# Forgetting-attention stages: weight splits in quarters, one a tile, and the square sums of queries and keys issued last at a tile's end

## The chip, the cores and the metric

One core of a Trainium2 chip runs the whole program. The metric is the device time of one execution in microseconds (us), the median of the runs. The engines, as the profile names them: PE (TensorE; PEld is its weight load), DVE (VectorE), ACT (ScalarE), POOL (GpSimd), SP (SyncE, which issues the weight transfers).

## What is computed

A first block of four layers works on 272 tokens (16 learned ones and 256 of the input) of width 1024, a second block of two layers on the 256. Layers 0 and 3 of the first block have the mixer that the change touches, "fox" in the names:

```python
def fox_mixer(h, w_in, b_f, q_gain, k_gain, w_out):
    proj = h @ w_in
    q, k, v, gate, f = jnp.split(proj, [D_MODEL, 2 * D_MODEL, 3 * D_MODEL, 4 * D_MODEL], axis=-1)
    q = rmsnorm(q.reshape(B, L, H, Dh), q_gain) * (Dh ** -0.5)      # 16 heads of 64
    k = rmsnorm(k.reshape(B, L, H, Dh), k_gain)
    c = jnp.cumsum(jax.nn.log_sigmoid(f + b_f), axis=1)
    # softmax(q k^T + c_q - c_k, causal) v, per head
    o = o * jax.nn.sigmoid(gate)
    return o @ w_out
```

All is fp32. The large products run as three products of rounded halves: weight and activation are each split into a high part (rounded to fp32r) and a low part (the rest), and high x high, high x low and low x high are summed in PSUM.

## The kernel before, in words

**Weights.** `stream()` lists the weight stages in order: `fox_in0` (8 blocks of 4 tiles), `fox_out0` (2 blocks), `gu0`, `dn0` and so on; `fox_in1` comes after `dn2`. A tile is 128 output features: 8 chunks of 128 rows, each with three matmuls of 128x272, 24 in all. A block is loaded in two halves of 2048 columns into a ring of four slots. ACT rounds a half into `ring_hi` (`split`, ACT's part, L1464), DVE subtracts and writes `ring_lo` (`split`, DVE's part, L1994). `hooks` decides when: a half of the next block at the tiles t with t % 4 = 0 and 2, so at every even tile. PE waits on `lo_ready` ahead of each half of a block.

**A fox_in stage.** `FOX_TILES` puts the 32 tiles in the order q, k, v of head pair 0, q, k, v of head pair 1, ..., then the 8 gate tiles. So head pair c has the tiles t = 3c (query), 3c + 1 (key) and 3c + 2 (value). Attention of the pairs is done between the tiles: five units a pair, called A (two, 144 keys), B (two, 272 keys) and M (16 learned tokens), in the slots 3c + 4, 3c + 5 and 3c + 6. Each engine has its own list in program order and none overtakes.

- PE, after tile t (`after`): the scores of the units in slot t; then, if tile t - 1 was a query or key tile, `statistic`, the sum of its squares over the 64 features of a head (the matmul `ps<-sq,con`); then `turn`, which transposes the probabilities of the units in slot t - 1; then `values`, their products with v, for slot t - 2. `statistic` writes PSUM bank 7, which holds one sum at a time: the one for keys waits on `head_ready`, that is until DVE is through with the query sum of the same pair. Half-way through a tile (`middle`) PE transposes a pair's values into the same bank.
- DVE, at tile t: `inverse` (reciprocals of slot t - 1); `head_norm` of tile t - 2 if it is a query or key tile (three `newton` steps L2010 to L2012 on `hrs`, then two products, L2092); the split hook; `evacuate` (tile t from PSUM times `rstd`, L2120); `largest` (row maxima of the scores of slot t, L2129).
- ACT, at tile t: `rstd_of` tile t - 2 (a logarithm and an exponential into `hrs`, L1464); copies of transposed probabilities (`take_turned`, slot t - 2) and of values (`take_tokens`); the split hook; the square of tile t; `exponent` of slot t. At tile 1 it also runs `log_sigmoid` with two table loads.
- POOL multiplies probabilities by the reciprocals.

At the end PE waits until the last gate tile has left PSUM (`all_read`) and goes on with `fox_out`. Two PSUM banks hold the tiles of this stage, so PE may start tile t + 2 only when tile t is evacuated.

## Time and profile before

| | |
|---|---|
| median of 3 runs | 2488.18 us (2487.27 to 2494.31) |
| profiled execution | 2484.18 us, span 2482.6 us |
| PE busy, share of the span | 93% |
| DVE, ACT, POOL busy | 63%, 49%, 25% |
| mean granted TensorE clock | 0.977 of full speed |
| first fox_in stage | PE starts at 23.05 us, the out stage at 205.89 us |
| second fox_in stage | ends at 1451.68 us |

Times in a timeline row are start and length of an instruction in us; what stands in brackets is how long the engine was idle just before it, and who ended that. PE's matmuls overlap, so starts tell its pace better than lengths.

### The profile page before, as it was taken

The numbers are of one execution on the slowest core, as the hardware profiler recorded it, in microseconds if no ns is written. First come the engines' busy times: TensorE is split into PE (matmuls) and PEld (weight loads), VectorE is DVE, ScalarE is ACT, GpSimd is POOL, SyncE is SP. The second block draws the span as 40 slices with busy tenths as digits, with TensorE's granted clock in tenths as the row PEclk, the third lists the DMA queues.
The fourth block names the chain that finished last, engine by engine and source line by source line (L and its number), as shares of the span: only waits on it lengthen the run. The fifth ranks groups of instructions, "written<-read, shape, count | busy, mean of one in ns | idle before, by whom it ended". The sixth has DMA issues, their size and how long they took to land. (4 is left out here: it accounts for less than half of the span.)

```text
span 2482.6 us, 47467 instructions
## 1 busy us (share of the span) xinstructions
PE 2303.6 (93%) x19122; PEld 2180.4 (88%) x19122; DVE 1555.4 (63%) x2514; ACT 1212.9 (49%) x1861; POOL 626.7 (25%) x774
## 2 busy tenths in 40 slices
PE   5999999999999898799989999997899998899998
PEld 4878999889999787699988789996788998788998
DVE  4665554746654764565556656546657975666994
ACT  4555544545444642355345554443446554456553
POOL 3114211013211030032121142216034535024550
PEclk9999999999999898899999999999999999999999
DMA  4324545324545212155442345454253554243554
GB/s 164 103 86 146 177 158 190 128 85 142 180 156 167 89 67 69 37 173 181 156 150 86 103 136 170 162 183 147 94 181 132 188 164 160 86 136 120 187 172 134
DMA packets 52859, 343.99 MB, mean 139 GB/s; under 512 B 5904, under 2 KB 7120, under 8 KB 20176
## 3 DMA queue, kind: packets, MB, share of 16 engines
q1 hardware_dynamic: 51984, 336.26, 41.0%
q0 software_dynamic: 704, 5.31, 0.5%
q8 instruction: 125, 2.05, 0.3%
q14 instruction: 46, 0.38, 0.0%
HBM read 340.43 MB, written 1.05 MB: 138 GB/s over the span
## 5 line engine op out<-in xcount | busy, mean ns | idle before, releaser
L740 PE MATMUL ps<-arena_r,ring_hi 128*128 128x272 f32 (+1 forms) x6688 | 1602.7, 289 | 16.8 <-DVE arena L2120 7.4
L740 PEld LDWEIGHTS ps<-arena_r,ring_hi 128*128 128x128 f32 x6688 | 1171.7, 191 | 26.8 <-issue 10.4
L740 PE MATMUL ps<-y_r,ring_hi 128*128 128x272 f32 (+1 forms) x3424 | 1019.9, 298 | 50.2 <-DVE ring_lo L1994 23.1
L740 PE MATMUL ps<-y_r,ring_lo 128*128 128x272 f32 (+1 forms) x3424 | 985.1, 288 | 0.0
L1994 DVE TENSOR_TENSOR ring_lo<-ring,ring_hi 128x2048 fp32r<-128x2048 f32 (+1 forms) x348 | 737.2, 2120 | 389.4 <-ACT ring_hi L1464 388.9
L740 PEld LDWEIGHTS ps<-y_r,ring_hi 128*128 128x128 f32 x3424 | 655.7, 192 | 79.5 <-issue 39.5
L740 PEld LDWEIGHTS ps<-y_r,ring_lo 128*128 128x128 f32 x3424 | 657.1, 192 | 0.0
L1464 ACT ACTIVATE ring_hi<-ring 128x2048 fp32r<-128x2048 f32 (+1 forms) x348 | 607.6, 1747 | 101.3 <-DMA ring<-dn 46.3
L740 PE MATMUL ps<-arena_r,ring_lo 128*128 128x272 f32 (+1 forms) x1632 | 468.3, 287 | 0.0
L740 PEld LDWEIGHTS ps<-arena_r,ring_lo 128*128 128x128 f32 x1632 | 310.1, 190 | 0.0
L1464 ACT ACTIVATE arena<-arena 128x272 f32<-128x272 f32 (+7 forms) x199 | 93.4, 472 | 404.1 <-DVE arena L2553 268.8
L2855 POOL CAST arena_r<-arena 128x272 fp32r<-128x272 f32 (+1 forms) x132 | 135.0, 1023 | 543.1 <-DVE arena L2555 420.2
L740 PE MATMUL ps<-arena 64*64 64x64 f32 (+16 forms) x2856 | 223.5, 264 | 21.7 <-DMA arena<-arena 6.1
L740 PEld LDWEIGHTS ps<-arena 64*64 64x64 f32 (+9 forms) x2856 | 160.8, 145 | 63.0 <-issue 34.6
L2863 POOL TENSOR_SCALAR arena<-x,par 128x272 f32<-128x272 f32 (+1 forms) x112 | 97.6, 871 | 380.7 <-ACT y_r L1464 380.0
L1464 ACT ACTIVATE sq<-x 128x272 f32<-128x272 f32 (+1 forms) x120 | 50.7, 423 | 236.7 <-DVE x L2032 236.7
L1464 ACT ACTIVATE arena<-ps 128x256 f32<-128x256 f32 (+7 forms) x299 | 92.7, 360 | 93.7 <-PE ps L740 37.1
L2032 DVE TENSOR_TENSOR x<-ps,x 128x272 f32<-128x272 f32 (+1 forms) x112 | 48.4, 432 | 100.2 <-PE ps L740 99.7
L2847 POOL CAST arena_r<-arena 128x256 fp32r<-128x256 f32 (+1 forms) x40 | 21.4, 534 | 335.0 <-DVE arena L2660 171.1
L2856 POOL TENSOR_TENSOR arena_r<-arena,arena_r 128x272 fp32r<-128x272 f32 (+1 forms) x132 | 103.0, 781 | 10.6
L1464 ACT ACT_TABLE_LOAD x69 | 88.5, 1283 | 23.1 <-DMA ring<-fox_in 9.3
L2594 DVE SCALAR_TENSOR_TENSOR arena<-arena,par 128x256 f32<-128x256 f32 x176 | 99.6, 624 | 0.0
(234 smaller groups left out, 1707.4 us busy)
## 6 DMA issues: line engine op xcount, KB each, us to landing
ring<-gu SPq DMA_DIRECT2D x88, 1024.0 KB, 5.0
ring<-dn SPq DMA_DIRECT2D x64, 704.0 KB, 4.0
ring<-up SPq DMA_DIRECT2D x44, 1024.0 KB, 5.0
ring<-fox_in SPq DMA_DIRECT2D x32, 1024.0 KB, 5.1
ring<-sdn SPq DMA_DIRECT2D x32, 704.0 KB, 4.0
ring<-gdn_in SPq DMA_DIRECT2D x16, 1024.0 KB, 5.0
ring<-in SPq DMA_DIRECT2D x16, 1024.0 KB, 5.1
ring<-gla_in SPq DMA_DIRECT2D x12, 1024.0 KB, 5.1
```

What stands on the lines that cost most here:

```text
L740: return nc.tensor.matmul(dst, w, mv, start=start, stop=stop)
L1464: return nc.scalar.activation(dst, src, f, **kw)
L1994: V.tensor_tensor(ring_lo[:, slot, 0:w], ring[:, slot, 0:w], ring_hi[:, slot, 0:w].bitcast(F32), ALU.subtract).then_inc(lo_ready, 1)
L2032: V.tensor_tensor(dst[:, c, :], take(c, width), dst[:, c, :], ALU.add).then_inc(evacuated, 1)
L2594: V.scalar_tensor_tensor(out=u_cc[:, q, :], in0=u_gp[:, q, 1 + tap:1 + tap + SEQ], scalar=par[:, bass.ds(i * 24 + (w0 + 12 * b + 3 * q + 1 ...
L2847: step(G.tensor_copy(hi_r[:, c, :], lo[:, c, :]))
L2855: step(G.tensor_copy(hi_r[:, c, :], lo[:, c, :]))
L2856: G.tensor_tensor(lo_r[:, c, :], lo[:, c, :], hi_r[:, c, :].bitcast(F32), ALU.subtract).then_inc(h_split, 1)
L2863: step(G.tensor_scalar(lo[:, c, :], src[:, c, :], pcol(gain, c), 1.0, ALU.mult, ALU.mult))
```

## The change

Fox_in stages split a quarter of a block (1024 columns) at every tile instead of a half (2048) at every even tile. All other stages still split halves. `hi_ready` and `lo_ready` now count quarters everywhere (a half counts two), and PE waits ahead of each quarter in all stages. In `after`, `statistic` moves behind `turn` and `values`.

```diff
+        def share(g, part):
+            w = half_width[g]
+            return slice(0, w) if part is None else slice(part * w // 2, (part + 1) * w // 2)
+        def quarters(at, part):
+            return 2 * at + (2 if part is None else part + 1)
-        def hooks(split, n, tpb):
+        def hooks(split, n, tpb, fine):
             def at(t):
                 g = n.block + t // tpb + 1
                 if g < len(half_width):
-                    if t % tpb == 0:
-                        split(g, 0)
-                    if t % tpb == tpb // 2:
-                        split(g, 1)
+                    if not fine:
+                        if t % tpb == 0:
+                            split(g, 0)
+                        if t % tpb == tpb // 2:
+                            split(g, 1)
+                    elif t % (tpb // 4) == 0:
+                        quarter = t % tpb // (tpb // 4)
+                        split(g, quarter // 2, part=quarter % 2)
...
-                            if at == 0:
-                                pe.wait_ge(lo_ready, i * (2 * turn) + (2 * (n.block + b) + half + 1))
+                            for part in range(2):
+                                if 0 <= at + P - 1 - part * width_of_half // 2 < P:
+                                    pe.wait_ge(lo_ready, i * (4 * turn) + quarters(2 * (n.block + b) + half, part))
...
                     for u in in_slot(units, t):
                         scores(u)
-                    if t:
-                        part, c = FOX_TILES[t - 1]
-                        if part in "qk":
-                            statistic(part, c)
                     for u in in_slot(units, t - 1):
                         turn(u)
                     slot = in_slot(units, t - 2)
                     if slot:
                         values(slot)
+                    if t:
+                        part, c = FOX_TILES[t - 1]
+                        if part in "qk":
+                            statistic(part, c)
...
-                fn(ring_hi[:, slot, 0:w], ring[:, slot, 0:w], ACT.Copy).then_inc(hi_ready, 1)
+                fn(ring_hi[:, slot, cols], ring[:, slot, cols], ACT.Copy).then_inc(hi_ready, 2 if part is None else 1)
...
-                before = hooks(split, n, tpb)
+                before = hooks(split, n, tpb, name.startswith("fox_in"))
...
-                V.tensor_tensor(ring_lo[:, slot, 0:w], ring[:, slot, 0:w], ring_hi[:, slot, 0:w].bitcast(F32),
-                                ALU.subtract).then_inc(lo_ready, 1)
+                V.tensor_tensor(ring_lo[:, slot, cols], ring[:, slot, cols], ring_hi[:, slot, cols].bitcast(F32),
+                                ALU.subtract).then_inc(lo_ready, 2 if part is None else 1)
...
-                after = hooks(split, n, tpb)
+                after = hooks(split, n, tpb, name.startswith("fox_in"))
```

On DVE, at tiles 11, 12 and the start of 13 of a fox_in stage, the list of before (line numbers of the kernel before; `newt` and `hrs` are `head_norm`, `raw` and the first `arena<-ps,rstd` are `evacuate`):

```order
89 L2092 SCALAR_TENSOR_TENSOR arena<-raw,gain,hrs 64x272 x2
90 L2120 TENSOR_TENSOR arena<-ps,rstd 128x272
...
98 L2012 SCALAR_TENSOR_TENSOR hrs<-newt,hrs 128x272
99 L2092 SCALAR_TENSOR_TENSOR arena<-raw,par,hrs 64x272 x2
100 L1994 TENSOR_TENSOR ring_lo<-ring,ring_hi 128x2048
101 L2120 TENSOR_TENSOR raw<-ps,rstd 128x272
...
104 L2139 RECIPROCAL row_inv<-row_sum 64x1
105 L2120 TENSOR_TENSOR raw<-ps,rstd 128x272
```

and of the changed kernel, where L2009 is the split and L2135 is `evacuate`:

```order
94 L2107 SCALAR_TENSOR_TENSOR arena<-raw,gain,hrs 64x272 x2
95 L2009 TENSOR_TENSOR ring_lo<-ring,ring_hi 128x1024
96 L2135 TENSOR_TENSOR arena<-ps,rstd 128x272
...
104 L2027 SCALAR_TENSOR_TENSOR hrs<-newt,hrs 128x272
105 L2107 SCALAR_TENSOR_TENSOR arena<-raw,par,hrs 64x272 x2
106 L2009 TENSOR_TENSOR ring_lo<-ring,ring_hi 128x1024
107 L2135 TENSOR_TENSOR raw<-ps,rstd 128x272
...
110 L2154 RECIPROCAL row_inv<-row_sum 64x1
111 L2009 TENSOR_TENSOR ring_lo<-ring,ring_hi 128x1024
112 L2135 TENSOR_TENSOR raw<-ps,rstd 128x272
```

One split of 2048 columns ahead of one of three evacuations has become a split of 1024 ahead of each.

On PE, at the end of tile 11, before and then after (`arena 128x272` are the scores B, L924 and L939 are `turn`, `arena 64x16` is `values` of M, `sq,con` is `statistic`):

```order
357 L740 MATMUL ps<-arena 128x272 x2
358 L740 MATMUL ps<-sq,con 128x272
359 L924 MATMUL ps<-con,arena 128x128
...
363 L740 MATMUL ps<-arena 64x16 x2
364 L740 MATMUL ps<-y_r,ring_hi 128x272
```

```order
357 L753 MATMUL ps<-arena 128x272 x2
358 L939 MATMUL ps<-con,arena 128x128
...
362 L753 MATMUL ps<-arena 64x16 x2
363 L753 MATMUL ps<-sq,con 128x272
364 L753 MATMUL ps<-y_r,ring_hi 128x272
```

The square sum, which stood directly behind the scores, now stands directly ahead of the next tile.

On DVE, at the last four gate tiles, before and then after (L2145 and L2160 multiply by the gate, L2150 and L2165 are a late split of the attention output):

```order
224 L1994 TENSOR_TENSOR ring_lo<-ring,ring_hi 128x2048
225 L2120 TENSOR_TENSOR arena<-ps,rstd 128x272
226 L2145 TENSOR_TENSOR arena<-arena 128x272 x5
227 L2120 TENSOR_TENSOR arena<-ps,rstd 128x272
228 L2145 TENSOR_TENSOR arena<-arena 128x272
229 L1994 TENSOR_TENSOR ring_lo<-ring,ring_hi 128x2048
230 L2120 TENSOR_TENSOR arena<-ps,rstd 128x272
231 L2145 TENSOR_TENSOR arena<-arena 128x272
232 L2150 TENSOR_TENSOR arena_r<-arena,arena_r 128x272
233 L2120 TENSOR_TENSOR arena<-ps,rstd 128x272
```

```order
238 L2009 TENSOR_TENSOR ring_lo<-ring,ring_hi 128x1024
239 L2135 TENSOR_TENSOR arena<-ps,rstd 128x272
240 L2160 TENSOR_TENSOR arena<-arena 128x272 x5
241 L2009 TENSOR_TENSOR ring_lo<-ring,ring_hi 128x1024
242 L2135 TENSOR_TENSOR arena<-ps,rstd 128x272
243 L2160 TENSOR_TENSOR arena<-arena 128x272
244 L2009 TENSOR_TENSOR ring_lo<-ring,ring_hi 128x1024
245 L2135 TENSOR_TENSOR arena<-ps,rstd 128x272
246 L2160 TENSOR_TENSOR arena<-arena 128x272
247 L2165 TENSOR_TENSOR arena_r<-arena,arena_r 128x272
248 L2009 TENSOR_TENSOR ring_lo<-ring,ring_hi 128x1024
249 L2135 TENSOR_TENSOR arena<-ps,rstd 128x272
```

A quarter now stands ahead of the last evacuation too, where no split stood.

## Rows read from the trace of the kernel before

**Rows 1.** The page, parts 1 and 5: busy time, and the split on DVE.

```profile
PE 2303.6 (93%) x19122; PEld 2180.4 (88%) x19122; DVE 1555.4 (63%) x2514; ACT 1212.9 (49%) x1861; POOL 626.7 (25%) x774
...
L1994 DVE TENSOR_TENSOR ring_lo<-ring,ring_hi 128x2048 fp32r<-128x2048 f32 (+1 forms) x348 | 737.2, 2120 | 389.4 <-ACT ring_hi L1464 388.9
```

**Rows 2.** PE's waits, 20 to 210 us: total, times, longest.

```profile
PE ps L740 <- DVE arena L2092: 9.1, 4, 2.8
```

**Rows 3.** PE's waits, 1277 to 1455 us (second stage), same columns.

```profile
PE ps L740 <- DVE arena L2092: 10.8, 4, 4.5
```

**Rows 4.** PE's timeline, the waiting square sums: start, length, instruction, idle before.

```profile
96.60 0.92 PE L740 MATMUL ps<-sq,con 128*128 128x272 f32 x2 [2.06 <-DVE arena L2092]
...
132.15 0.70 PE L740 MATMUL ps<-sq,con 128*128 128x272 f32 x2 [2.11 <-DVE arena L2092]
...
166.17 0.70 PE L740 MATMUL ps<-sq,con 128*128 128x272 f32 x2 [2.10 <-DVE arena L2092]
...
1343.90 0.70 PE L740 MATMUL ps<-sq,con 128*128 128x272 f32 x2 [2.12 <-DVE arena L2092]
...
1411.95 0.70 PE L740 MATMUL ps<-sq,con 128*128 128x272 f32 x2 [2.10 <-DVE arena L2092]
```

**Rows 5.** DVE's timeline, tiles 10 to 12 of the first stage.

```profile
89.25 2.29 DVE L1994 TENSOR_TENSOR ring_lo<-ring,ring_hi 128x2048 fp32r<-128x2048 f32 x1 [3.05 <-ACT ring_hi L1464]
91.46 0.43 DVE L2120 TENSOR_TENSOR raw<-ps,rstd 128x272 f32<-128x272 f32 x1
...
94.02 0.44 DVE L2010 SCALAR_TENSOR_TENSOR newt<-ps,hrs 128x272 f32<-128x272 f32 x1 [0.67 <-ACT hrs L1464]
...
96.49 0.44 DVE L2120 TENSOR_TENSOR arena<-ps,rstd 128x272 f32<-128x272 f32 x1
...
99.31 0.44 DVE L2010 SCALAR_TENSOR_TENSOR newt<-ps,hrs 128x272 f32<-128x272 f32 x1 [0.67 <-ACT hrs L1464]
...
102.02 2.29 DVE L1994 TENSOR_TENSOR ring_lo<-ring,ring_hi 128x2048 fp32r<-128x2048 f32 x1 [0.27 <-ACT ring_hi L1464]
```

**Rows 6.** ACT's timeline, the same stretch.

```profile
85.92 1.49 ACT L1464 ACTIVATE arena<-ps 128x256 f32<-128x256 f32 x6
87.32 1.90 ACT L1464 ACTIVATE ring_hi<-ring 128x2048 fp32r<-128x2048 f32 x1
91.93 0.43 ACT L1464 ACTIVATE sq<-raw 128x272 f32<-128x272 f32 x1 [2.71 <-DVE raw L2120]
...
105.33 0.94 ACT L1464 ACTIVATE arena<-ps 128x256 f32<-128x256 f32 x4
```

**Rows 7.** Timelines of ACT and DVE around a split of 1024 columns (stage in2b).

```profile
1746.45 1.04 ACT L1464 ACTIVATE ring_hi<-ring 128x1024 fp32r<-128x1024 f32 x1
...
1747.53 1.23 DVE L1994 TENSOR_TENSOR ring_lo<-ring,ring_hi 128x1024 fp32r<-128x1024 f32 x1 [1.43 <-ACT ring_hi L1464]
1748.67 0.41 DVE L2647 CUSTOM_DVE_ANT_0 arena<-ps,arena 128x256 f32<-128x256 f32 x1
```

**Rows 8.** Busy time by stretch: span, then PE, PEld, DVE, ACT, POOL, clock, DMA.

```profile
96.60:102.60 6.00, 6.00 (x34) 5.05 (x35) 4.27 (x13) 4.63 (x12) 0.98 (x2) 0.72 0.23 96
132.15:136.63 4.48, 4.48 (x34) 3.94 (x34) 3.04 (x11) 3.73 (x12) 0.99 (x2) 1.00 0.30 123
```

**Rows 9.** Timelines at a stage's start: DVE, ACT (first stage), DVE (both stages).

```profile
34.84 2.29 DVE L1994 TENSOR_TENSOR ring_lo<-ring,ring_hi 128x2048 fp32r<-128x2048 f32 x1 [0.29 <-ACT ring_hi L1464]
...
38.23 0.43 ACT L1464 ACTIVATE arena<-arena 16x272 f32<-16x272 f32 x1 [0.29 <-DVE arena L2081]
...
62.76 0.44 DVE L2120 TENSOR_TENSOR arena<-ps,rstd 128x272 f32<-128x272 f32 x1
...
1309.63 0.44 DVE L2120 TENSOR_TENSOR arena<-ps,rstd 128x272 f32<-128x272 f32 x1 [1.39 <-PE ps L740]
```

**Rows 10.** DVE's timeline, evacuation of gate tiles 28 and 31, first stage.

```profile
192.43 0.43 DVE L2120 TENSOR_TENSOR arena<-ps,rstd 128x272 f32<-128x272 f32 x1
...
205.41 0.42 DVE L2120 TENSOR_TENSOR arena<-ps,rstd 128x272 f32<-128x272 f32 x1
```

13 lines of the change are left out of this document (7 added, 6 removed).

## The prediction

> **What bounds the kernel now.** I read the busy shares first, then PE's waits in the two fox_in stages, then the timelines of PE, DVE and ACT there. PE is busy 93% of the span, DVE 63%, and the split on DVE is its largest group [rows 1]. So the kernel is bound by PE, and an edit that adds no PE work can win only where PE stands still. In the two stages that the change touches PE waits for `head_norm` (L2092) 9.1 and 10.8 us, four times each [rows 2, 3]. The first of the four comes at tile 2; the other three are 2.1 us each, always at a key sum, at tiles 11, 17 and 23, thus with every second head pair [rows 4].
>
> The three gaps recur at a fixed distance: 132.15 to 166.17 is 34.02 us, and 1343.90 to 1411.95 is two times 34.03 [rows 4]. PE's own work in such a stretch of six tiles is 34.02 - 2.10 = 31.92 us, 15.96 a head pair. The question that decides the prediction is whether only one late link makes the gap, or whether the whole round of DVE and ACT takes 34 us.
>
> I add the round up. DVE and ACT hand work to each other in program order, so each step is the distance between two starts. ACT's half 1.93 (87.32 to 89.25), DVE's half 2.21 (89.25 to 91.46), evacuation to the next one with a query `head_norm` between 5.03 (91.46 to 96.49) [rows 5, 6]; evacuation of the value tile to the next split 5.53 (96.49 to 102.02), which would be 2.82 + 2.47 = 5.29 if ACT's half were ready (96.49 to 99.31, and `head_norm` itself 94.02 to 96.49) [rows 5]; half 2.21; from there to ACT's copies 1.10 (105.33 less 104.23, where 104.23 is 102.02 + 2.21) [rows 5, 6]; copies 1.40 (85.92 to 87.32) [rows 6]. The next head pair has no split ahead of its key evacuation, which runs while ACT copies: 5.03 less the 0.47 from evacuation to square (91.46 to 91.93) is 4.56 [rows 5, 6]; then half 2.21, 5.29, 1.10 and 1.40. Sum 33.97 us. Measured are 34.02 and 34.03. **So in these stages the round between DVE and ACT sets the pace, not PE**, and the gap at each second key sum is only where PE notices. What was shortened at one place must shorten this sum, or PE waits elsewhere.
>
> **The change part by part.**
>
> *Quarters in the middle of a stage.* A quarter costs 1.08 us on ACT until DVE may start, and 1.14 on DVE (1746.45 to 1747.53 to 1748.67) [rows 7]. The new list has one ahead of each of the three evacuations. At the query and value tiles ACT's quarter is covered, since `head_norm` takes 2.47 us meanwhile; at the key tile, behind the copies, it is not. Round of one head pair: 1.08 + 1.14 + 5.03 + 1.14 + 5.29 + 1.14 + 1.10 + 1.40 = 17.32 us, two pairs 34.64. That is 0.62 longer than the 34.02 measured: two quarters cost 0.07 more than a half on DVE (three times), the key evacuation with its 0.47 is never free any more, and ACT's time on the path stays (2.16 against 1.93 + 0.24). The order that let one split per two pairs hide behind the tile's own wait is gone. PE then stands still 17.32 - 15.96 = 1.4 us in every pair instead of 2.1 in every second.
>
> *The square sum last.* It fills PE's wait with `turn` and `values`, and this would be a gain if PE set the pace. Under a round of DVE and ACT it moves work from behind the wait to before it and changes nothing but at tile 24, where the last round ends. Who waits for the later sum: ACT's `rstd_of`, for the query sum. ACT asks for it only behind the evacuation, the square and the exponents of the key tile, and that evacuation now stands 1.08 + 1.14 = 2.2 us behind ACT's copies, where it stood beside them. So I cost it at 0; bounds 0 and +0.5 a head pair, the latter if `values` still waits for ACT's copies when the sum is due.
>
> *From tile 5 to 23, first stage.* Evacuation at 62.76 [rows 9] to the one at 96.49 is 33.73, becomes 34.64: +0.91. 96.60 to 132.15 is 35.55, because the clock was at half speed for part of it: 6.00 us at a granted clock of 0.72 for what takes 4.48 at 1.00, so 1.5 us [rows 4, 8]. In the new round PE has 1.4 us to spare in a pair and such a spell costs about 0.1, so 34.64: -0.91. 132.15 to 166.17: +0.62. *Second stage.* At 1309.63 DVE waited 1.39 us for PE [rows 9], and the new quarter of 1.14 falls into that wait: 34.15 to 1343.78 becomes about 33.5, -0.6; then 68.05 becomes 69.28: +1.2.
>
> *Start of a stage.* DVE waited 0.29 for ACT's half at 34.84; with quarters it goes on at 34.55, evacuates at 35.69, ACT squares at 36.16, is free at 36.49, and has the quarter of tile 1, which did not stand there, until 37.56. The chain of `log_sigmoid` that started at 38.23 starts there: -0.67 [rows 5 to 7, 9]. It leads to PE's first key sum. I take the same in the second stage; bounds -1.2 and 0, since the quarter at tile 1 is queued ahead of that chain.
>
> *End of a stage.* From the evacuation of tile 28 to that of tile 31, on which `all_read` waits, are 12.98 us [rows 10]. Tile 28: a quarter in place of a half on both engines, 0.85 + 1.07, less 0.5 because ACT arrives later: -1.4. Tile 29: a new quarter on DVE, +1.14. Tile 30: -1.92. Tile 31: a quarter on both engines where none was, of which ACT's part is half covered, +1.6. Together -0.6 a stage, bounds -1.4 and +1.0.
>
> *More waits in PE's list.* Each half has one more wait, in all stages. The low part is written about a block ahead of its use, and in these stages PE's waits name `ring_lo` nowhere behind the first tile, so 0; bounds 0 and +1 us for the whole kernel. SP's transfers hang on PE's tiles and are not moved.
>
> The sum: first stage -0.67 + 0.91 - 0.91 + 0.62 - 0.6 = -0.65; second -0.67 - 0.6 + 1.2 - 0.6 = -0.65; together -1.3 us. Against the profiled execution this is 2484.18 - 1.3; the median of the runs stands 4.0 above that execution, so I put it on the median: **2486.9 us**. The terms' bounds give -5 to +5.
>
> **The rivals.**
>
> *The gaps close.* If the round had slack that my sum doesn't see, halving what stands ahead of the key evacuation brings `head_norm` forward by 0.85 + 1.07 = 1.9 us and the work now ahead of the sum fills the rest, so all six gaps of 2.1 go: -12.6, with the spell of half clock -1.5, starts -1.3, ends -1.2: 2471.6. For it: DVE is busy only 63%, and a half does stand ahead of the evacuation at 91.46, from which `head_norm` and the key sum at 96.60 follow [rows 4, 5]. Against it: the sum of the round meets the measured distance within 0.1 us, and the new round is longer. The Trainium skill, page "Perfetto Trace Analysis", section "Optimizing Scalar/DVE Operations", says that where Scalar and Vector are not saturated but cause bubbles elsewhere, breaking up instructions may let work complete sooner. By that rule this rival would be the forecast; by the rows, the pieces are all on the same path and their sum is what counts. The same section says that each instruction has a fixed overhead; the rows give that as 2 x 1.14 against 2.21. Chance 0.15.
>
> *Many small gaps cool PE.* The key sums of all pairs now wait, some eleven in the two stages instead of six. If each is followed by a spell of half clock as the one at 96.60 was, and PE cannot absorb it, each costs 1.5 us: ten more, +15, 2503. It decides where 15.96 + 1.52 = 17.48 passes the round of 17.32, so as I see it the price is 0.16 and not 1.5; and four of the five gaps in rows 4 show full pace behind them. It needs the spell to fall where DVE waits for PE. Chance 0.07.
>
> *The change does nothing.* Splits in quarters but the same round: within the forecast's range.
>
> **How the numbers follow.** Forecast 0.78, closing gaps 0.15, cooling 0.07. About 0.3%, 7.5 us, can be told from no change here. The forecast case lies between 2480 and 2494, the upper part for spells of half clock that fall otherwise in later stages. To hold 8 in 10 I stretch the low end into the first rival, to 2473. Faster: 0.15 and a small part of the forecast case, 0.18. Slower 0.07. Same 0.75.
>
> **What would show it.** Right: PE's waits for `head_norm` become six or more a stage of about 1.4 us and their sum stays near 9 us; key sums stand 17.3 us apart; each of DVE's quarters is 1.2 us. The distance from tile 5's evacuation to the sum at tile 23 grows. Wrong: key sums 16 us apart with no idle before them (closing gaps), or a granted clock under 1.00 behind most of them (cooling), or a wait for `ring_lo` that stood nowhere in these stages.

## The result: slower by 0.3%, through TensorE's granted clock

The changed kernel takes 2499.45 us (median of 20 runs, 2488.8 to 2509.54), the kernel before beside it 2492.99 (20 runs). The ratio is 1.0032, 95% interval 1.0018 to 1.0045. I had forecast no change, 2486.9 us, and gave 0.07 to slower. Of the 12.6 us between forecast and result 4.8 are the base: I had put the forecast on 2488.18, a median of three runs, where twenty give 2492.99. The rest is 1.3 us of gain that I had forecast and 6.5 us of loss.

The page of the changed kernel, part 1, and the two lists of PE's waits that answer to [rows 2] and [rows 3]: total, times, longest. The stretches are 20 to 210 and 1277 to 1465 us.

```profile
PE 2319.1 (93%) x19122; PEld 2198.3 (88%) x19122; DVE 1559.6 (62%) x2546; ACT 1215.1 (49%) x1893; POOL 627.0 (25%) x774
```

```profile
PE ps L753 <- DVE arena L2107: 6.0, 6, 2.6
PE ps L753 <- DVE arena L2135: 4.4, 2, 3.7
PE ps L939 <- ACT arena L1479: 3.8, 6, 0.7
```

```profile
PE ps L753 <- DVE arena L2107: 8.1, 6, 4.8
...
PE ps L939 <- ACT arena L1479: 3.5, 6, 0.7
```

PE issues the same 19122 matmuls as before [rows 1] but is busy 15.5 us longer. Its waits for `head_norm` (L2107, formerly L2092) are shorter than in [rows 2, 3], 6.0 and 8.1 us for 9.1 and 10.8, and new ones for ACT (3.8 and 3.5) stand beside them; all of PE's waits together come to 0.5 us more in the first stage and 1.2 us more in the second (18.3 to 19.5 from the key sum at tile 2 on). So the lost time is not idle time in the two stages that were changed. PE's timeline there, key sums of both stages, answers to [rows 4]:

```profile
96.58 0.70 PE L753 MATMUL ps<-sq,con 128*128 128x272 f32 x2 [0.68 <-DVE arena L2107]
101.12 0.85 PE L939 MATMUL ps<-con,arena 128*128 128x128 f32 x6 [0.66 <-ACT arena L1479]
113.75 0.70 PE L753 MATMUL ps<-sq,con 128*128 128x272 f32 x2 [0.67 <-DVE arena L2107]
130.93 0.70 PE L753 MATMUL ps<-sq,con 128*128 128x272 f32 x2 [0.69 <-DVE arena L2107]
148.10 0.70 PE L753 MATMUL ps<-sq,con 128*128 128x272 f32 x2 [0.68 <-DVE arena L2107]
165.26 0.70 PE L753 MATMUL ps<-sq,con 128*128 128x272 f32 x2 [0.66 <-DVE arena L2107]
```

```profile
1355.94 0.70 PE L753 MATMUL ps<-sq,con 128*128 128x272 f32 x2 [0.68 <-DVE arena L2107]
...
1424.62 0.70 PE L753 MATMUL ps<-sq,con 128*128 128x272 f32 x2 [0.67 <-DVE arena L2107]
```

Every pair now waits, and they stand 17.17 us apart: the round of DVE and ACT sets the pace, as argued. The time is lost elsewhere, in the stages named GLA and GDN here, the mixers of layers 1 and 2. Busy time by stretch: the program from PE's first matmul to the start of the GLA stage; then 132 matmuls at the start of that stage; then the stretch from the GDN stage to the end of that layer. Columns are span, PE busy (instructions), granted clock, DMA share, GB/s. First the kernel before, then the changed one:

```profile
23.06:435.28 412.22, 392.71 (x3025) 0.99 0.41 135
435.28:453.22 17.94, 17.94 (x132) 1.00 0.28 86
728.76:1120.22 391.46, 355.35 (x3803) 0.95 0.32 105
```

```profile
23.05:434.56 411.51, 391.48 (x3025) 0.99 0.41 136
434.56:454.05 19.49, 19.48 (x132) 0.91 0.24 73
731.28:1131.82 400.54, 363.61 (x3803) 0.92 0.31 102
```

Everything up to 435 us, with the first changed stage in it, has become 0.71 us shorter. Then come 132 matmuls of a stage that the diff leaves as it was but for its counting: the same work, no idle, 1.55 us longer at a granted clock of 0.91. The GDN stretch costs 9.1 us more at 0.92 against 0.95; this second difference will turn out to be scatter of single profiles. What the clock does there can be read in PE's timeline of the changed kernel, where the distance of the starts goes from 0.13 to 0.23 us with no wait in between, thus to the lower of the two levels (1.2 GHz for 2.4):

```profile
444.01 0.29 PE L753 MATMUL ps<-y_r,ring_lo 128*128 128x272 f32 x1
444.14 0.32 PE L753 MATMUL ps<-y_r,ring_hi 128*128 128x272 f32 x1
444.26 0.43 PE L753 MATMUL ps<-arena_r,ring_hi 128*128 128x272 f32 x1
444.48 0.43 PE L753 MATMUL ps<-y_r,ring_lo 128*128 128x272 f32 x1
444.71 0.43 PE L753 MATMUL ps<-y_r,ring_hi 128*128 128x272 f32 x1
```

**A measure for all runs.** A single profile can't carry a difference of 0.3% here, since the clock's low stretches fall differently in each execution. But every run reports its span and its mean granted clock. Their product is the time at full clock; the rest of the span I call *lost*. The clock is given to three places, worth 2.5 us, so only means count. And the split counts every stretch at the low clock as lost, also where PE would have waited for another engine anyway. One more run of the kernel before, 2598.92 us in a slower state, is left out. In the 151 others (five groups, each beside four or two of the experiments): full 2421.6 (standard error 0.25), lost 67.2 (0.6). The changed kernel: full 2421.0 (0.6), lost 76.7 (1.4). At full clock it is 0.6 us faster, within the error; it loses 9.5 us more to the clock. (The 20 runs of the kernel before that stand beside it have times alone on record, and their mean is 7.4 us under that of the changed kernel, in agreement within the errors.) So the whole loss is in the clock, and the question for the chip is which part of the change does it.

### The profile page after: what moved, and what is told of

It is laid out like the page before. It is cut to its first block and busy times, and to the rows that moved or that the text cites. A ratio compares the mean times of both kernels' runs of the same rounds, so it can differ in the third digit from the quotient of the medians.

```text
span 2500.6 us, 48406 instructions
## 1 busy us (share of the span) xinstructions
PE 2319.1 (93%) x19122; PEld 2198.3 (88%) x19122; DVE 1559.6 (62%) x2546; ACT 1215.1 (49%) x1893; POOL 627.0 (25%) x774
## 5 line engine op out<-in xcount | busy, mean ns | idle before, releaser
L753 PE MATMUL ps<-arena_r,ring_hi 128*128 128x272 f32 (+1 forms) x6688 | 1609.3, 290 | 16.6 <-DVE arena L2135 7.3
L753 PEld LDWEIGHTS ps<-arena_r,ring_hi 128*128 128x128 f32 x6688 | 1177.6, 192 | 27.4 <-issue 10.1
L753 PE MATMUL ps<-y_r,ring_hi 128*128 128x272 f32 (+1 forms) x3424 | 1027.6, 300 | 53.1 <-DVE ring_lo L2009 23.0
L2009 DVE TENSOR_TENSOR ring_lo<-ring,ring_hi 128x2048 fp32r<-128x2048 f32 (+2 forms) x380 | 742.4, 1955 | 412.5 <-ACT ring_hi L1479 411.0
L753 PE MATMUL ps<-y_r,ring_lo 128*128 128x272 f32 (+1 forms) x3424 | 990.6, 289 | 0.0
L753 PEld LDWEIGHTS ps<-y_r,ring_hi 128*128 128x128 f32 x3424 | 660.8, 193 | 81.8 <-issue 37.7
L1479 ACT ACTIVATE ring_hi<-ring 128x2048 fp32r<-128x2048 f32 (+2 forms) x380 | 613.6, 1615 | 110.8 <-DMA ring<-dn 50.3
L753 PEld LDWEIGHTS ps<-y_r,ring_lo 128*128 128x128 f32 x3424 | 662.8, 194 | 0.0
L753 PE MATMUL ps<-arena_r,ring_lo 128*128 128x272 f32 (+1 forms) x1632 | 468.9, 287 | 0.0
L753 PEld LDWEIGHTS ps<-arena_r,ring_lo 128*128 128x128 f32 x1632 | 310.6, 190 | 0.0
L753 PE MATMUL ps<-arena 64*64 64x64 f32 (+16 forms) x2856 | 224.7, 265 | 21.1 <-DMA arena<-arena 6.8
L753 PEld LDWEIGHTS ps<-arena 64*64 64x64 f32 (+9 forms) x2856 | 162.3, 145 | 62.4 <-issue 35.7
```

What stands on the lines that cost most here:

```text
L753: return nc.tensor.matmul(dst, w, mv, start=start, stop=stop)
L1479: return nc.scalar.activation(dst, src, f, **kw)
L2009: V.tensor_tensor(ring_lo[:, slot, cols], ring[:, slot, cols], ring_hi[:, slot, cols].bitcast(F32), ALU.subtract).then_inc(lo_ready, 2 if ...
```

## The experiments

The columns of this table: number of runs, ratio to the kernel before with its 95% interval, mean full and mean lost time in us (standard error of lost, 1.4 to 2.5).

| kernel | runs | ratio to before | full | lost |
|---|---|---|---|---|
| changed | 20 | 1.0032 [1.0018, 1.0045] | 2421.0 | 76.7 |
| e1 counting and extra waits | 11 | 1.0046 [1.0026, 1.0065] | 2421.2 | 78.2 |
| e2 changed, sums in the old place | 12 | 1.0031 [1.001, 1.0052] | 2420.8 | 73.8 |
| e3 sums last alone | 12 | 0.9988 [0.9972, 1.0004] | 2422.5 | 64.5 |
| e4 changed, extra waits in fox_in alone | 12 | 1.0022 [1.0004, 1.004] | 2422.2 | 71.3 |
| e5 before, one redundant wait a half | 12 | 1.0008 [0.999, 1.0027] | 2419.9 | 72.1 |
| e6 before, three redundant waits | 12 | 1.0001 [0.9982, 1.002] | 2420.1 | 69.5 |
| e7 counting alone | 9 | 1.0041 [1.0022, 1.0061] | 2421.9 | 76.9 |
| e8 changed, one wait a half | 12 | 1.0019 [0.9998, 1.0039] | 2421.5 | 71.0 |
| e9 lo_ready by twos | 12 | 1.0023 [1.0007, 1.0038] | 2420.7 | 75.7 |
| e10 hi_ready by twos | 12 | 0.999 [0.9972, 1.0008] | 2422.2 | 65.5 |
| e11 = e7 again | 12 | 1.0024 [1.0007, 1.0041] | 2424.4 | 71.4 |
| e12 changed, old counting | 10 | 0.9973 [0.9957, 0.999] | 2424.7 | 60.7 |
| e13 lo_ready and evacuated by twos | 7 | 1.0042 [1.0024, 1.0059] | 2423.3 | 76.8 |
| e14 evacuated by twos | 12 | 1.0038 [1.0023, 1.0054] | 2423.5 | 75.8 |
| e15 = e12 again | 12 | 0.9984 [0.9967, 1.0] | 2421.7 | 63.2 |
| e16 = e8 again | 12 | 1.0021 [1.0002, 1.0041] | 2421.4 | 72.5 |
| e17 lo_ready from an offset | 12 | 0.9994 [0.9981, 1.0007] | 2420.7 | 67.0 |
| e18 lo_ready by fours | 12 | 1.001 [0.9997, 1.0023] | 2422.4 | 69.6 |

### Which part of the change: e1 to e4

**e1**: the changed kernel with halves in all stages and the sums in the old place, so that only the counting in quarters and PE's extra waits are left.

```diff
-                before = hooks(split, n, tpb, name.startswith("fox_in"))
+                before = hooks(split, n, tpb, False)
...
-                after = hooks(split, n, tpb, name.startswith("fox_in"))
+                after = hooks(split, n, tpb, False)
```

> Halves everywhere and the old place of the square sums; only the counting in quarters and PE's additional waits are kept. Theory W (the additional waits in PE's list, which stand in all stages, cost time by themselves or by a lower granted clock in the mixer stages): 6 to 9 us slower than before, ratio near 1.003, and the mean clock 0.97 or less. Theory F (the loss comes from the fox_in stages alone): same as before within 2 us. Theory C (the later stages draw their spells of half clock by chance of timing, nothing in the change makes them more): same as before within 3 us.

**e2**: the changed kernel with `statistic` ahead of `turn` and `values` again.

```diff
+                    if t:
+                        part, c = FOX_TILES[t - 1]
+                        if part in "qk":
+                            statistic(part, c)
                     for u in in_slot(units, t - 1):
                         turn(u)
```

> Quarters and the additional waits, the square sums in their old place. By the sum of the prediction the round of a head pair stays 17.3 us, key sums 17.2 to 17.4 us apart, and the fox_in stages take what they take in the changed kernel, within 1 us. Theory W and theory F: 6 to 9 us slower than before. Theory C: within 3 us of before. If the place of the square sum matters after all: clearly different from the changed kernel.

**e3**: the kernel before with only the move of `statistic` behind `values`.

> Only the square sums moved; halves and waits as before. By the sum of the prediction the round of two head pairs stays 34.0 us and only tile 24 gains, 0.5 to 0.8 us a stage: 0 to -2 us. Theory W: same as before. Theory F, if the moved sums are what costs: 6 us or more slower.

**e4**: the changed kernel; blocks of the fox_in stages keep their two waits a half, all others wait once, for both quarters.

```diff
-                                if 0 <= at + P - 1 - part * width_of_half // 2 < P:
-                                    pe.wait_ge(lo_ready, i * (4 * turn) + quarters(2 * (n.block + b) + half, part))
+                                if n.block + b in in_quarters:
+                                    if 0 <= at + P - 1 - part * width_of_half // 2 < P:
+                                        pe.wait_ge(lo_ready, i * (4 * turn) + quarters(2 * (n.block + b) + half, part))
+                                elif at == 0 and part == 0:
+                                    pe.wait_ge(lo_ready, i * (4 * turn) + quarters(2 * (n.block + b) + half, 1))
```

> The changed kernel, but PE waits twice a half only for the blocks that are split in quarters; elsewhere once a half as before. Theory W: 6 to 9 us faster than the changed kernel, so 1 to 2 us faster than before. Theory F: like the changed kernel, 6 to 9 us slower than before. Theory C: within 3 us of before.

Measured: e1, which works in the fox_in stages exactly like the kernel before, has the whole loss, 78.2 us. e3, which has no new counting, has none. So the quarters and the late sums are not needed for the loss; the line of the diff that I had costed at nothing, counting and waits, is enough. e4 came out between the two and settled nothing. For the round, PE's timelines of e2 and then of e3 are worth reading:

```profile
96.78 0.70 PE L753 MATMUL ps<-sq,con 128*128 128x272 f32 x2 [1.17 <-DVE arena L2107]
...
113.95 0.70 PE L753 MATMUL ps<-sq,con 128*128 128x272 f32 x2 [1.18 <-DVE arena L2107]
```

```profile
101.00 0.70 PE L740 MATMUL ps<-sq,con 128*128 128x272 f32 x2 [1.46 <-DVE arena L2092]
...
135.10 0.70 PE L740 MATMUL ps<-sq,con 128*128 128x272 f32 x2 [1.44 <-DVE arena L2092]
```

With the sum in its old place the quarters give the same 17.17 us a pair (e2). With the sum late and halves as before, two pairs take 34.10 (e3) against 34.02 in [rows 4]. The late sum shortens the gap named at the key sum and does nothing for the round.

### The waits or the counting: e5 to e8

Theory W: the extra waits on PE lower the clock. Theory C: the counting by twos does.

**e5, e6**: the kernel before with one, and with three, redundant waits in each half, for a value that PE has already seen. This is e5; e6 has four parts in place of two.

```diff
-                            if at == 0:
-                                pe.wait_ge(lo_ready, i * (2 * turn) + (2 * (n.block + b) + half + 1))
+                            for part in range(2):
+                                if 0 <= at + P - 1 - part * (tpb * kc * P // 2) // 2 < P:
+                                    pe.wait_ge(lo_ready, i * (2 * turn) + (2 * (n.block + b) + half + 1))
```

> The kernel before with one redundant wait more on PE in the middle of each half of weights, for the same value of the semaphore that PE has already seen; counting, splits and sums as before. Of each run's time I take the span times the mean granted clock (the time at full clock, 2422.0 us for the kernel before) and what is left over (lost to the clock, 66.8 us before, 76.7 in the changed kernel). Theory W, the extra waits on PE take the clock down: lost 74 to 79 us, ratio to before 1.003 to 1.005. Theory C, the counting in quarters (increments of two, doubled values, other register arithmetic) does it: lost 64 to 69, ratio 0.999 to 1.001.

> The kernel before with three redundant waits more in each half. Theory W: more than with one, lost 80 to 100 us if the loss goes with the number of waits, ratio 1.006 to 1.014; 74 to 79 if one wait already does all of it. Theory C: lost 64 to 69, ratio 0.999 to 1.001. If the time at full clock grows too, a wait costs time of its own: up to 1 us by my prediction.

**e7**: e1 without its extra waits; **e8**: the changed kernel without them. Both have this at PE:

```diff
-                            for part in range(2):
-                                if 0 <= at + P - 1 - part * width_of_half // 2 < P:
-                                    pe.wait_ge(lo_ready, i * (4 * turn) + quarters(2 * (n.block + b) + half, part))
+                            if at == 0:
+                                pe.wait_ge(lo_ready, i * (4 * turn) + quarters(2 * (n.block + b) + half, 1))
```

> Halves and sums as in the kernel before, PE waits once a half as before, but the semaphores count quarters: each half adds two, and every value waited for is doubled. Theory W: lost 64 to 69 us, ratio 0.999 to 1.001. Theory C: lost 74 to 79 us, ratio 1.003 to 1.005.

> The changed kernel with its quarters and its late sums, but PE waits once a half, for the half's second quarter, in all stages. Theory W: the changed kernel without its loss: time at full clock 2421 us, lost 64 to 69, ratio to before 0.998 to 1.000, thus about where my prediction put the changed kernel. Theory C: lost 74 to 79, ratio 1.003, as the changed kernel. Either way the key sums of the fox_in stages stand 17.17 us apart, as in the changed kernel.

Measured: three redundant waits a half change nothing (1.0001), and one hardly anything (1.0008); the time at full clock is lower than before by 1.5 us, not higher. The counting without any extra wait has the loss, 76.9. So theory W has fallen as the cause of the whole. A share of a few us is not excluded: e5 lost 72.1 where the kernel before beside it lost 68.0, and e8, the changed kernel without the extra waits, lies between the groups at 71.0 against 76.7.

### Which semaphore, and can the change be had without it: e9 to e12

**e9** and **e10**: the kernel before with one of the two semaphores counted by twos, `lo_ready` (from DVE to PE) or `hi_ready` (from ACT to DVE). e9:

```diff
-                                pe.wait_ge(lo_ready, i * (2 * turn) + (2 * (n.block + b) + half + 1))
+                                pe.wait_ge(lo_ready, i * (4 * turn) + 2 * (2 * (n.block + b) + half + 1))
...
-                                ALU.subtract).then_inc(lo_ready, 1)
+                                ALU.subtract).then_inc(lo_ready, 2)
```

> The kernel before in which only lo_ready counts by twos: DVE's split adds two, PE waits for twice the value, and the register that PE multiplies for it in its loops is one of its own. Lost to the clock (span less span times mean granted clock) was 67 to 68 us in the kernel before and 76.9 with both semaphores doubled. If PE's own list of waits and register work is the cause (theory P), this kernel has all of it: lost 74 to 79, ratio 1.003 to 1.005. If it is the counting on ACT and DVE (theory D): 65 to 70, ratio 0.999 to 1.001. If the counting isn't a cause and e7 and e1 were drawn high by chance: 65 to 70 here, in the next kernel and in the third.

> The kernel before in which only hi_ready, between ACT and DVE, counts by twos; PE's list is word for word that of the kernel before. Theory P: lost 65 to 70 us, ratio 0.999 to 1.001. Theory D: 74 to 79, ratio 1.003 to 1.005.

**e11** is e7 once more.

> The kernel with the counting alone once more, on another day's runs and perhaps another chip, since single kernels differ in twelve runs by a standard error of 2 us. If counting lowers the clock: lost 74 to 79 us again, ratio 1.003 to 1.005, and a spell of half clock about 9 us into the first GLA stage, which the profiles of four kernels without the new counting don't have. If it was chance: lost 65 to 71.

**e12**: the changed kernel with its quarters and late sums, with PE's line and the values of both semaphores as in the kernel before. The first quarter of a half has a semaphore of its own between ACT and DVE and signals nothing to PE.

```diff
-                fn(ring_hi[:, slot, cols], ring[:, slot, cols], ACT.Copy).then_inc(hi_ready, 2 if part is None else 1)
+                fn(ring_hi[:, slot, cols], ring[:, slot, cols], ACT.Copy).then_inc(hi_first if part == 0 else hi_ready, 1)
...
-                v.wait_ge(hi_ready, i * 8 + quarters(at, part))
+                if part == 0:
+                    firsts.append(at)
+                    v.wait_ge(hi_first, len(firsts))
+                else:
+                    v.wait_ge(hi_ready, i * 4 + (at + 1))
...
+                if part != 0:
+                    low.then_inc(lo_ready, 1)
```

> The changed kernel with its quarters and late sums, but the old counting and PE's old waits: the first quarter of a half is signalled between ACT and DVE by a semaphore of its own, and only the second one counts for lo_ready. If the counting is the whole of the loss (P or D): time at full clock 2421 us, lost 65 to 70, total within 2486 to 2491, ratio 0.998 to 1.000, which is what I predicted for the changed kernel. If the quarters or the late sums cool PE too: lost above 72, ratio above 1.001.

Measured: `hi_ready` is innocent (65.5), `lo_ready` alone has the loss (75.7). e11 repeats e7 with a smaller loss, 71.4, between the two ranges that I had given. e12 is the opposite of the changed kernel with the same quarters and late sums: 0.9973, lost 60.7, lower than the 65 to 70 that I had expected. Its rows, key sums first, then the three stretches from above:

```profile
97.38 0.70 PE L754 MATMUL ps<-sq,con 128*128 128x272 f32 x2 [0.67 <-DVE arena L2115]
114.54 0.70 PE L754 MATMUL ps<-sq,con 128*128 128x272 f32 x2 [0.66 <-DVE arena L2115]
```

```profile
22.91:434.90 411.99, 393.14 (x3025) 0.98 0.41 135
434.90:452.83 17.93, 17.93 (x131) 1.00 0.29 90
728.49:1120.06 391.57, 355.30 (x3802) 0.95 0.32 105
```

The same pairs of 17.16 us, the same gaps of 0.67; but the GLA stage's first matmuls run at full clock again, and the GDN stretch is at 391.6.

### What it is in the counting: e13 to e18

Doubling `lo_ready` also changes PE's compiled list in the looped stages: by the traces PE executes 296 register instructions for 312. **e13** doubles `evacuated`, the other semaphore of these loops, as well, which brings back the 312 (e18 has them too); **e14** doubles `evacuated` alone.

```diff
-                        pe.wait_ge(evacuated, i * (turn * tpb) + (n.tile + t + 1 + BANKS - banks))
+                        pe.wait_ge(evacuated, i * (2 * turn * tpb) + 2 * (n.tile + t + 1 + BANKS - banks))
...
-            v.sem_inc(evacuated, BANKS)
+            v.sem_inc(evacuated, 2 * BANKS)
```

and every `then_inc(evacuated, 1)` adds two.

> The kernel before in which lo_ready and evacuated both count by twos. In PE's compiled list the register and wait instructions of the looped stages are then in the places of the kernel before again (three in 51 rows), where the doubling of lo_ready alone gave another list (two in 50 rows). If PE's list is the cause (theory R): lost to the clock 65 to 70 us, ratio 0.999 to 1.001, no spell of half clock 9 us into the first GLA stage. If the increments of two on lo_ready are (theory I): lost 74 to 79, ratio 1.002 to 1.005, the spell there.

> The kernel before in which only evacuated counts by twos; PE's list has the register and wait instructions of the kernel before. Theory R and theory I: lost 65 to 70 us, ratio 0.999 to 1.001, no spell in the first GLA stage. If any semaphore counted by twos does it: 74 to 79.

**e15** and **e16** are e12 and e8 once more.

> The kernel with quarters, late sums and the old counting once more, to see whether its gain holds: if the recounting was the whole loss, 0.998 to 1.000 with 65 to 70 us lost; in the first twelve runs it was 0.9973 with 60.7 lost, which is lower than any cause that I know of explains. No spell in the first GLA stage.

> The changed kernel with one wait a half once more. It has the register code of the looped stages that goes with lo_ready doubled, but its one profile had no spell at the start of the first GLA stage and its loss was 71.1 us, between the groups. If that code or counting lowers the clock: 72 to 78 lost, ratio 1.002 to 1.004. If the extra waits on PE of the changed kernel have a part: 65 to 70.

**e17**: `lo_ready` starts at an offset, so it has the large values but increments of one. **e18**: it counts by fours.

```diff
-                                pe.wait_ge(lo_ready, i * (2 * turn) + (2 * (n.block + b) + half + 1))
+                                pe.wait_ge(lo_ready, i * (2 * turn) + (len(half_width) * 2 + 2 * (n.block + b) + half + 1))
...
             v.sem_inc(evacuated, BANKS)
+            v.sem_inc(lo_ready, len(half_width) * 2)
```

```diff
-                                pe.wait_ge(lo_ready, i * (2 * turn) + (2 * (n.block + b) + half + 1))
+                                pe.wait_ge(lo_ready, i * (8 * turn) + 4 * (2 * (n.block + b) + half + 1))
...
-                                ALU.subtract).then_inc(lo_ready, 1)
+                                ALU.subtract).then_inc(lo_ready, 4)
```

> The kernel before in which lo_ready starts at the number of all halves and then counts by ones: as large values as with the doubling, increments of one, PE's list unchanged in form. If large values are the cause (theory V): lost to the clock 72 to 78 us, ratio 1.002 to 1.005, a spell of half clock 9 us into the first GLA stage. If increments of more than one are (theory I): lost 63 to 70, ratio 0.999 to 1.001, no such spell.

> The kernel before in which lo_ready counts by fours; PE's list has the same kinds of instructions in the same places as in the kernel before. Theory I: lost 72 us or more, with the spell in the first GLA stage; if the loss goes with the size of the increment, 85 us or more, ratio 1.006 and up. Theory V: the same, since the values are larger still. If what counts is only that PE's register instructions stood elsewhere (which the kernel with both semaphores doubled spoke against): lost 63 to 70, ratio 0.999 to 1.001.

Measured: with the old list and both semaphores doubled the loss is all there (76.8), so it isn't the register instructions. `evacuated` alone does it too (75.8), against both theories that I had named. The repeats: e15 has a gain again, smaller (0.9984, lost 63.2, below the 65 to 70 expected), and e16 lost 72.5, at the lower end of what the counting should give, above the 65 to 70 of the extra waits. Large values with increments of one do nothing (67.0). That left the increments; but by fours the loss is 69.6, ratio 1.001, and not the 72 or more that I asked for. So the size of the increment doesn't set it, and the increments as the cause are not shown.

**What an increment of more than one does to the program.** It is not only a number. The trace of the kernel before has no semaphore instruction at the line of the split's wait (L1993); those of e9 and e18 have 348 there, one for each split. The wait for `hi_ready`, which was part of the split, has become an instruction of its own ahead of it. Here are the first lines of the pages of the kernel before, e17, e9 and e18:

```profile
span 2482.6 us, 47467 instructions
```

```profile
span 2486.7 us, 47468 instructions
```

```profile
span 2499.0 us, 47791 instructions
```

```profile
span 2499.7 us, 47807 instructions
```

It costs time. ACT's half and DVE's split in the timelines of e9:

```profile
88.13 1.90 ACT L1464 ACTIVATE ring_hi<-ring 128x2048 fp32r<-128x2048 f32 x1
...
90.13 2.29 DVE L1994 TENSOR_TENSOR ring_lo<-ring,ring_hi 128x2048 fp32r<-128x2048 f32 x1 [2.98 <-ACT ring_hi L1464]
```

The split starts 0.10 us after ACT's half has ended (88.13 + 1.90), where the kernel before has 0.03 (87.32 + 1.90 to 89.25, [rows 5, 6]). So it is in all eleven profiles with `lo_ready` by twos or fours (the quarters of the fox_in stages, which add one, apart) and in none of the nine others. In the fox_in stages it shows as a longer round, 34.09 to 34.13 us for two head pairs in e1, e7, e9, e11 and e18, where no low clock falls into it, against 34.02. A doubled `evacuated` (e14) puts such waits ahead of DVE's evacuations, a doubled `hi_ready` (e10) ahead of ACT's rounding. This leaves a rival to "a semaphore that PE waits on": that DVE's work comes some hundredths of a us later. e10 fits both, for its semaphore is one that PE doesn't wait on and that DVE doesn't send. e18, which has the same delay with hardly any loss, speaks against either as the whole cause. No run separates them.

One sign goes with `lo_ready` by twos or fours: whether the first 132 matmuls of the GLA stage run at 0.91. Here are these stretches of e7, e18, e17 and e15, in this order:

```profile
437.17:456.66 19.49, 19.49 (x132) 0.91 0.25 79
```

```profile
437.12:456.59 19.47, 19.47 (x131) 0.91 0.27 87
```

```profile
435.90:453.84 17.94, 17.94 (x132) 1.00 0.31 95
```

```profile
436.49:454.42 17.93, 17.93 (x131) 1.00 0.28 91
```

Ten of the eleven profiles with `lo_ready` counted by twos or fours show the slow stretch there, and none of the nine others. The exception is e8, at 1.00, while e16, the same kernel, has it. These 132 matmuls are worth 1.55 us of the 8 to 10; the whole GLA stage is worth more. From the issue of its first weights to that of the first of the MLP behind it, the kernel before and the changed one:

```profile
419.05:568.71 149.66, 137.23 (x1023) 0.97 0.34 113
```

```profile
418.01:571.24 153.23, 140.32 (x1023) 0.94 0.33 110
```

In the eleven profiles this stage takes 148.8 to 153.2 us, 151.5 on the mean, in the nine others 145.0 to 149.9, on the mean 148.2. These 3.3 us are the one part of the loss that the traces can place, and even they don't follow the loss throughout: e18 has them (152.3) with hardly any loss, e14 its loss without them (149.9). The GDN stage can't be told apart in the same way: from its first weights to those of the MLP behind it the eleven have 280.2 us on the mean and the nine 280.0. The changed kernel's 288.6 is their longest; e14 has 288.3, and all others lie between 276.5 and 284.3. So the 9.1 us of the GDN stretch in the first comparison are scatter of a single profile.

## Why the prediction was wrong, point by point

**The pace of the fox_in stages: right.** The round was to be 17.32 us a pair and is 17.17. Its evacuations are read off DVE's timeline of the changed kernel (tiles 10 to 13):

```profile
91.43 0.43 DVE L2135 TENSOR_TENSOR raw<-ps,rstd 128x272 f32<-128x272 f32 x1
...
97.60 0.43 DVE L2135 TENSOR_TENSOR arena<-ps,rstd 128x272 f32<-128x272 f32 x1
...
104.03 0.43 DVE L2135 TENSOR_TENSOR raw<-ps,rstd 128x272 f32<-128x272 f32 x1
```

```profile
107.46 1.23 DVE L2009 TENSOR_TENSOR ring_lo<-ring,ring_hi 128x1024 fp32r<-128x1024 f32 x1 [2.05 <-ACT ring_hi L1479]
108.60 0.43 DVE L2135 TENSOR_TENSOR raw<-ps,rstd 128x272 f32<-128x272 f32 x1
```

6.17 is 5.03 + 1.14, and 6.43 is 5.29 + 1.14, as in the sum. The last piece is 4.57 where I had 1.10 + 1.40 + 1.08 + 1.14 = 4.72: ACT's copies take 1.26, not 1.40. These are ACT's copies and quarter of the pair before:

```profile
87.95 1.35 ACT L1479 ACTIVATE arena<-ps 128x256 f32<-128x256 f32 x6
89.21 1.04 ACT L1479 ACTIVATE ring_hi<-ring 128x1024 fp32r<-128x1024 f32 x1
```

So the rival in which the gaps close was rightly kept small. In it I had named the Trainium skill's rule that breaking up instructions may let work complete sooner ("Perfetto Trace Analysis", "Optimizing Scalar/DVE Operations"). By the rows the 17.17 us of a pair, 34.34 for two, stand against 34.02 in [rows 4]: the pieces delayed each other on the same path.

**The square sum last: right at 0.** e2 and the changed kernel have the same 17.17. Its bound named the reason: `values` still waits for ACT's copies. The gain at tile 24 that I had seen is there in e3, which takes 38.5 us from tile 23's evacuation to tile 31's for 39.4, but e3 also takes 34.8 from tile 5's to tile 11's for 34.2, so a stage gains next to nothing. The forecast single gap of 1.4 shows as two of 0.67 a pair, one at L939 for ACT and one at L753 for `head_norm`. The waits of both kinds add up to 9.8 us in the first stage, where I had put about 9.

**Start and end: the links were right, the terms were not.** `log_sigmoid` begins at 37.63 and not at 38.23 [rows 9], -0.60 for -0.67. The last gate tile is evacuated at 204.39 and not at 205.41 [rows 10], and the out stage starts 1.0 us earlier; I had -0.65 for the whole stage. These are ACT's and DVE's rows:

```profile
37.63 0.43 ACT L1479 ACTIVATE arena<-arena 16x272 f32<-16x272 f32 x1
```

```profile
204.39 0.43 DVE L2135 TENSOR_TENSOR arena<-ps,rstd 128x272 f32<-128x272 f32 x1
```

But the -0.60 didn't last to tile 5. Taken apart at DVE's evacuations, before to after, in us, the stages are:

| piece | forecast, first, second | first stage | second stage |
|---|---|---|---|
| PE's first matmul to tile 5 | -0.67, -0.67 | 39.70 to 40.21, +0.51 | 33.60 to 34.81, +1.21 |
| tile 5 to 11 | +0.91, -0.6 | 33.73 to 34.34, +0.61 | 34.16 to 34.59, +0.43 |
| tile 11 to 23 | -0.29, +1.2 | 69.56 to 68.69, -0.87 | 68.05 to 68.68, +0.63 |
| tile 23 to 31 | -0.6, -0.6 | 39.36 to 38.10, -1.26 | 39.36 to 38.09, -1.27 |

The first stage's sum of -1.0 for -0.65 is thus in good part luck: start and end are off by +1.2 and -0.7 us, the two pieces between by -0.3 and -0.6. Its -0.87 holds because the kernel before lost 1.5 us to half clock in that piece and the changed kernel runs at 1.00 there; I had the spell return and be absorbed. One sign that I had named for being right, that the distance from tile 5's evacuation to the sum at tile 23 grows, is against me: it falls from 103.41 to 102.00 us, and in the second stage from 102.32 to 102.24. (The late sum now stands ahead of its tile's quarter and evacuation; from evacuation to evacuation the second stage's distance grows by 1.1 us and the first one's falls by 0.3.)

**The second stage: wrong by 1.6 us.** Before and after, from PE's key sum at tile 2 to the start of the out stage, in the columns of the stretches above:

```profile
1290.63:1451.68 161.05, 147.07 (x1127) 0.97 0.30 98
```

```profile
1302.18:1464.23 162.05, 147.29 (x1127) 0.96 0.29 97
```

I had -0.65 and it is +1.00. PE stands still 0.8 us longer (14.76 for 13.98), and the clock is a little lower. The table puts it at the start: +1.21 where I had taken over -0.67. The key sum at tile 2 stands where it stood (14.61 us behind the stage's first matmul, 14.60 before), and then PE waits for POOL's transfer of the cumulative sums `c` at tile 4, 3.50 us for 2.90, until 13.12 us after that key sum where it was 11.96. So DVE's wait for PE at tile 5, into which I had let the new quarter fall, is gone, 0.16 for the 1.39 in [rows 9]:

```profile
1322.38 0.44 DVE L2135 TENSOR_TENSOR arena<-ps,rstd 128x272 f32<-128x272 f32 x1 [0.16 <-PE ps L753]
```

Whether the change does this isn't shown: from tile 0 to tile 5 the second stage takes 28.2 us in e12 and 30.5 in e15, which are the same kernel.

Together, the sum of -1.3 us is to be held against the time at full clock: 2421.0 (0.6) for 2421.6, and 2421.7 (1.1) and 2424.7 (0.9) in e15 and e12. The two stages as profiled sum to 0.0. It lies within the scatter of these means; the runs can't confirm a gain of 1 us.

**"More waits in PE's list": the step that failed.** I costed the line of the diff that touches every stage at 0 with bounds of 0 and +1 us, from the observation that PE waits for `ring_lo` nowhere. That observation holds after the change too: PE's waits for it come to 23.5 us, three times, in both kernels. And the waits themselves cost no time at full clock (e5, e6). But I looked at the waits and not at the other half of that edit, the counting, and I gave the whole term a bound that priced only delays. Even as a delay it wasn't nothing: 316 of the changed kernel's 380 splits, the halves, start 0.07 us later behind ACT. What counts for the time is the granted clock: where I had 0 the changed kernel loses 9.5 us more to it. e7, which has the counting and nothing else, is 8.9 us over the kernels before beside it in the lost part of its first nine runs (76.9 for 68.0), and 5.0 in e11 (71.4 for 66.4).

**"Many small gaps cool PE": right level, wrong place.** This rival had the clock as mechanism, 2503 as its time and 0.07 as its chance. But it wanted the low clock behind the gaps of the fox_in stages. Up to 435 us the granted clock is 0.99 in both kernels, from tile 5 to tile 31 it is 1.00 in both stages of the changed one, and e12 with the same gaps is faster than the kernel before. The gaps don't do it.

**The range.** My 2473 to 2494 allowed for "spells of half clock that fall otherwise in later stages", but only as scatter about the median of the kernel before. A shift of their mean was not in it, and neither was an error of the base: 2494 lies 5.8 us over the 2488.18 that I started from and 1.0 over the 2492.99 of twenty runs.

**What is shown, and what is open.** Shown: the loss is time at the lower clock; it needs neither the quarters, nor the late sums, nor the extra waits (e7, e9); the change without its recounting doesn't have it (e12, e15); large values are not the cause (e17), and the places of the register instructions are not (e13). Supported by repeated runs, but not shown to be the cause: the doubling of `lo_ready` (e9) or of `evacuated` (e14), with the wait of its own that it puts into DVE's list. Increments of two predict the groups but fail at fours. Open: how either comes to lower TensorE's clock. A wider reading, that any edit which shifts fine timing moves the mean loss by several us, isn't excluded: e5, which has no doubling, lies at 72.1, above e8, e11 and e4, which have it. Against chance alone stands that all eleven series with a doubling of these two semaphores, repeats included, lie above the mean of the kernel before, by 4 to 11 us. The other eight lie between -7 and +5, among them e18 at +2, which by its edit belongs to the first.

**The version to use.** e12 is the faster of all: 2487.42 us (10 runs) and 2485.72 (12 runs, e15), ratios 0.9973 [0.9957, 0.999] and 0.9984 [0.9967, 1.0]. The changed kernel is at 1.0032, so e12 gains 0.5 to 0.6% over it, about 12 to 15 us; it leaves out both the recounting and the extra waits, and e8 and e16 (1.0019 and 1.0021), which leave out the waits alone, gain 0.1%. Its small gain over the kernel before is in the lost part (62 for 67), not at full clock. The traces offer a reason why the quarters could give it. From tile 5's evacuation to that of tile 31 the seven profiles with quarters take 141.1 to 141.7 us in all 14 stages, and one of these has a spell of low clock. The thirteen with halves take 141.5 to 147.6 in 26 stages, 143.0 on the mean, and nine of them hold such a spell and take 142.6 us or more. That is 1.7 us a stage and 3.4 in both. Kernels with recounting fit as well: with halves they lose 75.8 us on the mean (e1, e7, e9, e11, e13, e14), with quarters 73.1. It is a pattern read after the fact, and no run was made to test it.

## What to carry to other kernels

An edit that touches every stage, even by a changed count in a wait that never waits, deserves a wider bound than the stage that it is meant for: PE's clock can take back 0.3% through it. Keep the counting of shared semaphores as it is, in increments of one, and give a new fine-grained signal a semaphore of its own: here an increment of two or four took the wait out of the instruction that carried it and made it start 0.07 us later. Count the instructions on the first line of the two pages before a change of counting is called free. When a kernel is bound by TensorE and an expected 0.1% is at stake, split each run into time at full clock and time lost to it before any reason is looked for, and take twelve runs or more.

## What the runs showed that I had not expected

Time lost to the granted clock is 2.7% of this kernel, 67 us, and varies between single runs of the same program more than anything that the edit does: the kernel before ran from 2476.86 to 2503.82 us in 151 runs, while its time at full clock has a standard error of 0.25 us. The same 132 matmuls, without an idle between them, take 17.94 us at a clock of 1.00 and 19.49 at 0.91. The granted clock moved with a change that alters no matmul and no transfer and delays DVE's splits by 0.07 us: 0.9693 on the mean in the changed kernel, 0.9692 with the doubled counts alone (0.9714 in their repeat), 0.9730 in the kernel before. For one part of it the traces show the place, the GLA stage, but not the reason.
